# X and T products of an inversion level side by side in the RWKV part, filling pieces behind both, norm products at other levels

## What is computed

```
def rwkv7_time_mix(z, mu, w0, w_up, a0, a_up, g_up, k_k, k_a, r_k, ln_w, ln_b):
    z = z + (z_prev - z) * mu
    r, k, v, lw, la, lg = jnp.split(z, ...)
    decay = jnp.exp(-math.exp(-0.5) * jax.nn.sigmoid(w0 + jnp.tanh(lw) @ w_up))
    a = jax.nn.sigmoid(a0 + la @ a_up)
    ...
    def step(state, inp):
        r_t, w_t, k_t, v_t, ka_t, kb_t = inp
        sa = jnp.einsum('bhvk,bhk->bhv', state, ka_t)
        state = (state * w_t[:, :, None, :] + sa[..., None] * kb_t[:, :, None, :]
                 + v_t[..., None] * k_t[:, :, None, :])
        y_t = jnp.einsum('bhvk,bhk->bhv', state, r_t)
        return state, y_t
    _, y = lax.scan(step, s0, xs)
    mean = jnp.mean(y, axis=-1, keepdims=True)
    var = jnp.mean(jnp.square(y - mean), axis=-1, keepdims=True)
    yn = (y - mean) * lax.rsqrt(var + RW_GN_EPS) * ln_w + ln_b
    bonus = jnp.sum(r * kf * r_k, axis=-1, keepdims=True) * v
    out = (yn + bonus) * g
```

## Time and profile before

| | |
|---|---|
| time, median of 3 runs | 3882.52 us (3879.24 to 3888.97) |
| profiled execution: its time | 3883.28 us |
| profiled execution: its span | 3880.9 us |
| granted TensorE clock, mean | 0.992 |
| PE busy | 3752.1 us (97%) |
| DVE busy | 1767.7 us (46%) |
| ACT busy | 1469.0 us (38%) |
| POOL busy | 1126.8 us (29%) |
| chain that ended last, share of PE | 88% |

### The profile page before, as it was taken

How to read it: one execution, slowest core, us unless ns; L and a number is a source line. 1 busy time by engine, 2 the same in 40 slices (tenths; PEclk the granted TensorE clock), 3 DMA queues, 4 the chain that set the end, 5 groups by cost and what they waited for, 6 DMA issues and landing times.

```text
span 3880.9 us, 60252 instructions
## 1 busy us (share of the span) xinstructions
PE 3752.1 (97%) x25676; PEld 3010.7 (78%) x25676; DVE 1767.7 (46%) x2777; ACT 1469.0 (38%) x2362; POOL 1126.8 (29%) x639
## 2 busy tenths in 40 slices
PE   8989999999999999999999999999999999999998
PEld 6966778888887578888667788788876777887886
DVE  4266433333354743435856423444368563234333
ACT  3356332222344643332453233433335433334333
POOL 0010222222301033331332236433413322363333
PEclk9999999999999999999999999999999999999999
DMA  5113133322113122222111122223221101222222
GB/s 221 66 52 131 66 125 104 120 73 70 64 66 122 38 96 98 93 87 87 60 39 40 35 87 98 95 92 104 87 82 55 50 30 40 98 103 87 98 96 78
DMA packets 60201, 323.30 MB, mean 83 GB/s; under 512 B 6048, under 2 KB 6176, under 8 KB 34080
## 3 DMA queue, kind: packets, MB, share of 16 engines
q1 hardware_dynamic: 59936, 319.46, 23.5%
HBM read 317.34 MB, written 2.10 MB: 82 GB/s over the span
## 4 chain that ended last, share of the span: by engine, by line
PE 88%; DVE 6%; ACT 3%; issue 1%; DMA 1%; SPq 0%; POOL 0%; DVEq 0%; ACTq 0%; POOLq 0%
PE ps L1584 54%; PE ps L1595 4%; PE ps L756 4%; PE ps L787 3%; PE ps L2630 3%; PE ps L2259 2%; PE ps L1083 2%; PE ps L3132 1%; PE ps L1118 1%; PE ps L2705 1%; PE ps L2727 1%; PE ps L1098 1%; PE ps L2725 1%; PE ps L2247 1%; PE ps L1130 1%
## 5 line engine op out<-in xcount | busy, mean ns | idle before, releaser
L1970 DVE SCALAR_TENSOR_TENSOR ftmp<-ps,vec,ftmp 128x511 f32<-128x511 f32 (+2 forms) x440 | 301.7, 694 | 321.6 <-ACT ftmp L1924 206.3
L1556 POOL TENSOR_TENSOR PWL<-ring,PWH 128x1024 fp32r<-128x1024 f32 (+2 forms) x114 | 260.6, 2286 | 638.6 <-ACT PWH L1542 638.6
L1556 POOL TENSOR_TENSOR WL<-ring,WH 128x1024 fp32r<-128x1024 f32 (+3 forms) x102 | 226.9, 2224 | 598.3 <-ACT WH L1542 598.3
L1542 ACT ACTIVATE PWH<-ring 128x1024 fp32r<-128x1024 f32 (+2 forms) x216 | 211.8, 982 | 431.7 <-PE ps L1584 390.2
L1542 ACT ACTIVATE WH<-ring 128x1024 fp32r<-128x1024 f32 (+3 forms) x160 | 158.7, 993 | 531.0 <-PE ps L1584 500.0
L1584 PE MATMUL ps<-FH,WH 128*128 128x512 f32 x1008 | 305.7, 357 | 0.0
L1584 PE MATMUL ps<-FH,WL 128*128 128x512 f32 x1008 | 305.1, 357 | 0.0
L1584 PE MATMUL ps<-FL,WH 128*128 128x512 f32 x1008 | 303.5, 355 | 0.0
L1556 POOL TENSOR_TENSOR PW3L<-ring,PW3H 128x1024 fp32r<-128x1024 f32 (+2 forms) x90 | 204.1, 2267 | 271.2 <-ACT PW3H L1542 271.1
L1549 DVE TENSOR_TENSOR PWL<-ring,PWH 128x1024 fp32r<-128x1024 f32 (+2 forms) x102 | 117.6, 1155 | 334.2 <-ACT PWH L1542 334.1
L1584 PEld LDWEIGHTS ps<-FH,WH 128*128 128x128 f32 x1008 | 166.1, 188 | 35.6 <-issue 7.4
(11 more groups left out here) (623 smaller groups left out, 9689.6 us busy)
## 6 DMA issues: line engine op xcount, KB each, us to landing
ring<-in_wup SPq DMA_DIRECT2D x88, 1024.0 KB, 4.7
ring<-in_wgate SPq DMA_DIRECT2D x24, 1024.0 KB, 4.7
ring<-in_wada SPq DMA_DIRECT2D x22, 1024.0 KB, 4.8
ring<-in_wdown SPq DMA_DIRECT2D x24, 896.0 KB, 4.6
adab<-in_wada SPq DMA_DIRECT2D x40, 512.0 KB, 5.6
ring<-in_win SPq DMA_DIRECT2D x18, 1024.0 KB, 4.7
ring<-in_wout SPq DMA_DIRECT2D x16, 1024.0 KB, 4.8
ring<-in_wdown SPq DMA_DIRECT2D x12, 1024.0 KB, 5.0
```

The costliest lines, as they stand in the source:

```text
L1542: e.activation(wh, view, ACT.Copy).then_inc(*whi_a.up(L, n))
L1556: e.tensor_tensor(wl, view, wh.bitcast(F32), SUB).then_inc(*wlo_g.up(L, n))
L1970: e.scalar_tensor_tensor(out=dst, in0=src, scalar=conv_cols(L, ch, a), in1=dst, op0=MUL, op1=ADD).then_inc(*(ffn_v.up(L, "tap", x, j, c) i ...
```

## The change

PE no longer runs a filling piece between the X and the T products of a level: both pieces stand behind T (behind RB and RK in level 1). PE's `fin` step, so `mean` and `var`, moves from behind X to the end of its level, and DVE's `fin` step from a level's start to its end. ACT's order stays as it was. `BACK` follows the new order, which moves some PSUM banks. `gate_free` drops the wait of the first gates for pair 2's output `o`, and keeps it for gate 7.

```
-        BACK = (... + level(1, "X") + [("W1", 1), ("mean", 1)] + level(1, "T")
-                + [("RB", 2), ("RK", 2)] + level(2, "X") + [("var", 1)] + level(2, "T") + [y for lv in range(3, 6) for x in "XT" for y in level(lv, x)]
+        BACK = (... + level(1, "X") + [("W1", 1)] + level(1, "T")
+                + [("RB", 2), ("RK", 2), ("mean", 1)] + level(2, "X") + level(2, "T") + [("var", 1)] + [y for lv in range(3, 6) for x in "XT" for y in level(lv, x)]
...
@@ tensor_rwkv, back
                         mm.then_inc(*rw_mm.up(L, pp, "W1"))
-                    next(fin, None)
-                    yield 1
                     for h in range(2):
                         pr = back_ps(("T", lv, h))
...
                     if lv == 1:
                         gram("RB", bt, rt, rt_)
                         gram("RK", kt, rt)
+                    next(fin, None)
+                    yield 1
                     yield 1
@@ gate_free
-            return [rw_v.at(L, 3, "G"), rw_v.at(L, 2, "o"), *([own[c]] if c in own else [])]
+            return [rw_v.at(L, 3, "G"), *([rw_v.at(L, 2, "o")] if c == 7 else []), *([own[c]] if c in own else [])]
```

More of the change, by code:

```diff
@@ L2506, in level @@
             return [((x, lv, h), 1) for h in range(2)]
-        BACK = ([("TM", 2), ("AT", 2)] + [(f"tok{i}", 1) for i in range(4)] + [("AK", 2)] + level(1, "X") + [("W1", 1), ("mean", 1)] + level(1, "T")
-                + [("RB", 2), ("RK", 2)] + level(2, "X") + [("var", 1)] + level(2, "T") + [y for lv in range(3, 6) for x in "XT" for y in level(lv, x)]
+        BACK = ([("TM", 2), ("AT", 2)] + [(f"tok{i}", 1) for i in range(4)] + [("AK", 2)] + level(1, "X") + [("W1", 1)] + level(1, "T")
+                + [("RB", 2), ("RK", 2), ("mean", 1)] + level(2, "X") + level(2, "T") + [("var", 1)] + [y for lv in range(3, 6) for x in "XT" for y in level(lv, x)]
                 + [("MN", 2), ("DP", 2), ("E", 2)] + [(("S", c), 1) for c in range(1, 7)] + [("Y", 2), ("YS", 1)])
```

## The result

The changed kernel took 3892.88 us in the median of 18 runs (3886.7 to 3902.21), the kernel before 3884.6 in 18 runs (3879.24 to 3891.07). The ratio is 1.0018, 95% interval 1.0012 to 1.0025: slower, by less than the 0.3% that I called no change. The forecast's sum was +8.5 us on the profiled execution, 3891.8, and it was given as 3891.5; the medians differ by 8.3, and the ratio's interval reaches from 4.7 to 9.7 us.

A forecast was written before the change was run, and what follows sets the result against it. PE, busy 97% of the span, was taken to bound the kernel. From 3883.28 us, gains of 4.8, 0.4 and 2.3 against waits of 9.8 and 1.7 gave +4.0, the clock +4.5: 3891.8, stated as 3891.5, range 3884 to 3898.

The forecast's parts named there:

- Part 1 and 2: PE, levels 2 to 5: adjacent pieces gain 0.19 to 0.27, uncovered X to T loses 0.08; net 0.15 a level, 4.8 us.
- Part 3: Last pair, before T of level 4: dropping the gate's wait removes PE's 1.14 us wait in both layers, gaining 2.3.
- Part 4: Level 1, first k quarter: PE waits for lw, 2.44 us four times (9.8) and 0.83 twice in pair 0 (1.7).
- Part 5: Behind the four 2.44 us waits: three lower PE's clock to 1.2 GHz, costing 1.5 us each, 4.5 in all.
- All four: Behind the four waits for lw: by the skill's clock rule every one lowers the clock, making the sum 3893 us.
- the 2.31: An earlier PE wait in the profile, 2.31 us, with full clock behind it; by that row the sum would be 3887.
- 2 (the clock stays, or falls once): Rival: the waits for lw come but lower the clock at most once, 3887.3 to 3888.8 us; chance 0.22.
- 3 (no wait): Rival at level 1's k quarters: lw is early, PE doesn't wait, only gains remain, 3875.8 us; chance 0.05.
- 4 (ACT late at X): Rival at X to T: T's first half starts only after both ACT copies, 15 us more, 3907; chance 0.08.
- 5, a pause behind each table load: Rival in the four waits: each table switch holds ACT another 1.28 us, 5.1 more, 3896.9; chance 0.04.
- the drain of 1.38: ACT's table switches: by the skill each of the four waits would be 1.38 us longer, 5.5 in all.
- the forecast of the joints: Forecast for e1: X to X takes 6.12 in place of 6.29 in levels 2 to 4, 5.1 us less.

The follow-up runs named there:

- e7: The unaltered change run again as a control, against the kernel before: 3892.68 us, ratio 1.0024.
- e1: The change with level 1 put back as before (first filling piece and mean between W1 and T): 3882.47 us, ratio 0.9986 to the kernel before.
- e8: The change with ACT's two copies of X in the other order in levels 2 to 5: 3921.19 us in one run.
- e3: The kernel before with only level 1 and the norm product mean as in the change: 3898.31 us, ratio 1.0027 to the kernel before.
- e5: The change with mean and DVE's subtraction back behind W1 in level 1, both pieces still behind T: 3883.11 us, ratio 0.9997 to the kernel before.
- e6: The change with ACT's filling step (table load, lw, AA, table load) ahead of Square in level 1: 3879.74 us, ratio 0.9988 to the kernel before.
- e4: The change plus 8 unread matmuls where PE waits for lw in pairs 1 and 2: 3889.68 us, ratio 1.0010 to the kernel before.
- e11: The same kernel as e4, run again on another chip: 3886.94 us, ratio 1.0010 to the kernel before.
- e2: The kernel before with only the gate's wait for pair 2's output dropped: 3881.61 us, ratio 0.9983 to the kernel before.
- e10: The same kernel as e2, run again on another chip: 3879.32 us, ratio 0.9987 to the kernel before.
- e9: The same kernel as e1, run again on another chip: 3877.47 us, ratio 0.9984 to the kernel before.

## Why the prediction was right

**Part 1 and 2, joints and hand-over.** T 1.16 to 1.17 behind X against 1.15; two pieces 2.94 to 2.96 against 2.94 to 3.02; net 0.12 to 0.17 a level against 0.15. The prediction's 6.29 "as in all undisturbed levels" holds for two levels; the others take 6.27 or 7.12, with no effect on the sum. The sum is 4.7 by the change's profile and 5.5 by e7's, against 5.2. e1's stage, 5.2 below before, shows the gain without the loss, and e8 shows what the hand-over hangs on. ACT was on time at every X, at level 4 too.

**Part 3, the gate.** The two waits of 1.14 went, as worked out.

**Part 4, the wait for `lw`.** Four waits of 2.38 against 2.44, two of 0.77 against 0.83. The chain was that of the forecast, link by link: the quarter starts 4.56 behind `mean`, as worked out. Each wait came out 0.06 shorter because PE itself was busy for 2.18 of these 4.56 in place of 2.12; four of them make 0.25 us. e3 has the whole loss without the rest of the change, e1 the rest without the loss, e5 and e6 break the chain at two different links with the same wait of 0.77 left over.

**Part 5, the clock.** I took three falls of four at 1.5 us. The change's profile has two, e7 and e3 three, e8 four: 12 of 16. The price of one fall came out as 1.5 too. "All four", the 3893 that the prediction has "by the rule", was its own reading: the Trainium skill (TensorE: Matmul & The Clock Gate, HAM oscillation) tells of waits for DMA longer than these. And the 2.31 that stayed at full clock was no rule either, as the last section shows. That the clock falls there only behind a bare wait is shown by e4, e11, e5 and e6: waits of 0.40 and 0.77 at those places and no fall behind any of sixteen (pairs 1 and 2 in both layers of four profiles). Whether a given bare wait lowers it differs from run to run, and no run shows what decides it. What the falls cost in the mean is less sure than the three of four: by the mean clocks under "What stays open" it is about 4.2 us in e7 and nothing in e3, each uncertain by some 2.

**The rivals.** 2 (the clock stays, or falls once) is in none of the four profiles, which have two to four falls; single runs of it are not ruled out, since each of these four profiles is of one execution. 3 (no wait) fell by the trace. 4 (ACT late at X) fell by the 1.16. 5, a pause behind each table load, fell by 2072.01 - 2070.72 = 1.29 in the change's row (and Square ends at 2070.70, so there is none ahead of the load either), and with it the drain of 1.38 that the Trainium skill (ScalarE: Activation LUTs, What ACT_TABLE_LOAD costs) gives: with it the waits would be 3.8.

**What I had not counted.** The issue waits of PE, in front of the gram products and transposes at the head of a pair. They make 5.7 us in the stages before and 7.8 in the change's profile, but 5.2 in e7's, so they are not part of the effect; they move the single profile.

**How near it came.** That 8.5 met 8.3 is in part luck. The mechanism is shown, but the ratio leaves 4.7 to 9.7 us open, e7 gave 1.0024 (9.3 us), and the number of falls varies from run to run.

**What stays open.** Dropping the gate's wait alone gave 0.9983 and 0.9987, 6.6 and 5.0 us, where the trace shows 2.3 in the two waits. The clock that each run lists can account for the surplus.

Over the 86 runs of the kernel before that stood beside the experiments, a run whose mean granted clock is 0.001 higher is 2.3 us shorter. e2's runs averaged 0.9921 against 0.9910 beside them, e10's 0.9918 against 0.9911, worth 2.6 and 1.7 us. Their means are 4.9 and 4.0 us below before, so 2.3 and 2.3 are left, the two waits. The same estimate leaves 4.8 us for e1 and 5.5 for e9, which is 2.5 and 3.2 more than for e2 and e10. The stages say 4.8 and 3.1 (439.0 and 440.0 against 443.8 and 443.1), the forecast of the joints said 5.1. For e7 it leaves 4.7 us of loss without the clock, where the forecast had 4.0.

It is an estimate after the fact, from clocks listed to 0.001, and each of its differences is uncertain by some 1.7 us; why e2's and e10's runs had the higher clock no run shows. Without it, the medians don't tell e1 and e2 apart (3882.47 and 3881.61, then 3877.47 and 3879.32). They do show that e1 is below the kernel before in both comparisons (upper ends 0.9995 and 0.9992), and below the change.

## What to carry to other kernels

When work is moved so that two pieces of filling stand together, look at what the second piece waits for: here it needed the answer of another engine to the first, and the products that used to stand between them were its cover. Follow the answering engine's queue too, since an instruction moved on one engine can hold up, on another, an unrelated one behind its consumer. Turning round two steps on that other engine (e6) can be worth as much as undoing the move.

## What the runs showed of the hardware

TensorE's clock fell behind quite short waits. It went to 0.50 for 3.4 us behind 12 of 16 waits of 2.38, and behind issue waits of 3.01, 3.00, 2.29, 2.18, 2.03, 1.88, 1.84, 1.71 and once of 1.42, but not behind others of 1.86, 1.83 and 1.80; it never fell behind 0.40 or 0.77 at the places of `lw`. Nor is it the place: in the parts that no edit touches, the wait of 2.03 of the earlier trace rows lowered it in 9 of the 13 profiles, that of 2.31 in 11 (not in the kernel before, whose row the prediction used, nor in the change) and that of 2.83 in all 13; one of 2.55 at about 2930 did in 5. So the length of the wait alone does not decide, and one trace does not tell whether a wait costs the clock. A fall costs about 1.5 us of dense work, so a wait of this kind is priced at its length and up to 1.5 more.

An issue wait can belong to a kernel's list of instructions: the two runs of e4 stood 3.01 and 3.00 at one and the same instruction, a transpose of pair 2, while the change's profiles have 1.06 and 0.96 at the head of that pair. The two kernels differ by the added matmuls only. The length does not repeat everywhere: at the head of pair 1 the change has 1.86 in one profile and 1.30 in the other. I did not test what makes these waits or why the added matmuls move them.
